# Splitting the weights of the mLSTM stage: seven subtractions moved from GpSimd to VectorE, and the modulation steps placed anew

## The reference

```
def mlstm_mixer(h, w_in, conv_w, b_if, hnorm_g, w_out):
    proj = einsum('bsd,de->bse', h, w_in)               # 1024 qk, 1024 v, 1024 o, 16 gate columns
    qk = silu(causal_conv(qk, conv_w))                  # four taps
    q, k = split(qk, 2)
    i_pre, f_pre = split(gates + b_if, 2)
    log_f = log_sigmoid(f_pre)                          # running sums and maxima give the decay
    ...
    hh = num / max(abs(den), exp(-m_t))                 # per head, from q, k, v and the decay
    hh = rmsnorm(hh, hnorm_g) * sigmoid(o)
    return einsum('bse,ed->bsd', hh, w_out)
```

## Time and profile before

| | us |
|---|---|
| median of 3 runs | 2704.84 (2700.52 to 2705.44) |
| the profiled execution, its time | 2700.52 |
| its span | 2698.4 |
| PE busy | 2605.1 |
| DVE busy | 2003.0 |
| ACT busy | 1506.9 |
| POOL busy | 346.0 |

### The profile page before, as it was taken

One profiled execution on the slowest core, in us unless ns is written; L12 is line 12 of the kernel. 1 busy time (PEld: TensorE's weight loads), 2 busy tenths in 40 slices (PEclk: granted clock), 3 DMA queues, 4 the chain that ended last, 5 costly groups with the idle time before them and its releaser, 6 DMA issues.

```text
span 2698.4 us, 48877 instructions
## 1 busy us (share of the span) xinstructions
PE 2605.1 (97%) x17298; PEld 2380.5 (88%) x17298; DVE 2003.0 (74%) x3797; ACT 1506.9 (56%) x2604; POOL 346.0 (13%) x190
## 2 busy tenths in 40 slices
PE   5999999999999999899999999999999999999998
PEld 4779999999888888789999999888888889888897
DVE  6768957888888876568857888666666776677766
ACT  3455557766565656455557766665664544463443
POOL 3107600000000002607600000000000111002000
PEclk9999999999999999999999999999999999999999
DMA  6844574444788874424574444555555345542553
GB/s 223 292 144 164 195 230 147 141 147 148 267 277 278 280 257 142 143 70 165 195 231 141 146 144 149 187 195 193 191 193 190 105 166 194 180 156 96 194 187 132
DMA packets 134718, 490.78 MB, mean 182 GB/s; under 512 B 15521, under 2 KB 15609, under 8 KB 134273
## 3 DMA queue, kind: packets, MB, share of 16 engines
q1 hardware_dynamic: 131904, 480.31, 52.5%
q0 software_dynamic: 2624, 7.92, 0.9%
HBM read 487.12 MB, written 1.06 MB: 181 GB/s over the span
## 4 chain that ended last, share of the span: by engine, by line
PE 86%; DVE 7%; ACT 3%; DMA 2%; issue 2%; POOL 0%; SPq 0%; DVEq 0%; ACTq 0%; POOLq 0%
PE ps L221 77%; PE ps L1295 4%; DMA weight_ring<-in_stream 2%; ACT weight_split L236 1%; DVE weight_split L245 1%; PE ps L640 1%; DVE arena L1821 1%; DVE arena L632 1%; ACT arena L395 1%; PE ps L2402 1%; PE ps L1267 1%; DVE arena L1817 1%; POOL weight_split L245 0%; PE ps L1708 0%; PE ps L388 0%
## 5 line engine op out<-in xcount | busy, mean ns | idle before, releaser
L221 PE MATMUL ps<-hT_split,weight_split 128*128 128x256 f32 x9984 | 1260.1, 285 | 15.9 <-DVE hT_split L1831 4.7
L221 PEld LDWEIGHTS ps<-hT_split,weight_split 128*128 128x128 f32 x9984 | 1220.0, 192 | 27.5 <-issue 18.3
L245 DVE TENSOR_TENSOR weight_split<-weight_ring,weight_split 128x1024 fp32r<-128x1024 f32 x674 | 823.6, 1223 | 399.3 <-ACT weight_split L236 396.6
L236 ACT ACTIVATE weight_split<-weight_ring 128x1024 fp32r<-128x1024 f32 x800 | 848.0, 1061 | 230.5 <-PE ps L221 160.2
L221 PE MATMUL ps<-weight_split,hidden_split 128*128 128x512 f32 x3948 | 913.1, 390 | 7.3 <-DVE hidden_split L1561 3.6
L221 PEld LDWEIGHTS ps<-weight_split,hidden_split 128*128 128x128 f32 x3948 | 735.4, 188 | 160.0 <-issue 8.1
L245 POOL TENSOR_TENSOR weight_split<-weight_ring,weight_split 128x1024 fp32r<-128x1024 f32 x126 | 306.2, 2436 | 413.9 <-ACT weight_split L236 413.6
L1391 ACT ACTIVATE hidden_split<-arena 128x256 fp32r<-128x256 f32 (+1 forms) x256 | 176.3, 689 | 252.3 <-PE ps L221 252.3
L1383 ACT ACTIVATE arena<-ps 128x256 f32<-128x256 f32 (+18 forms) x248 | 126.9, 512 | 133.8 <-PE ps L221 133.8
L221 PE MATMUL ps<-weight_split,hT_split 128*128 128x512 f32 x660 | 159.9, 398 | 10.6 <-POOL weight_split L245 5.6
L1561 DVE TENSOR_TENSOR hidden_split<-arena,hidden_split 128x256 fp32r<-128x256 f32 x256 | 161.3, 631 | 0.0
(11 more groups left out here) (351 smaller groups left out, 1716.3 us busy)
## 6 DMA issues: line engine op xcount, KB each, us to landing
weight_ring<-in_stream SPq DMA_DIRECT2D x912, 512.0 KB, 3.3
x<-in_x SPq DMA_DIRECT2D x1, 1024.0 KB, 4.9
arena<-mlstm_m_rows POOLq DMA_DIRECT2D x1, 1024.0 KB, 6.4
arena<-in_ln_mix_g POOLq DMA_DIRECT2D x2, 512.0 KB, 4.9
arena<-in_ln_mix_b POOLq DMA_DIRECT2D x2, 512.0 KB, 6.1
arena<-in_ln_ffn_g POOLq DMA_DIRECT2D x2, 512.0 KB, 4.8
arena<-in_ln_ffn_b POOLq DMA_DIRECT2D x2, 512.0 KB, 6.4
out<-x SPq DMA_DIRECT2D x2, 512.0 KB, 2.6
```

What stands on the lines that cost most here:

```text
L221: mm = pe.matmul(out_, stationary(s_part), moving(m_part), start=start and n == 0, stop=stop and n == 2, skip_group_check=True)
L236: act.activation(wsplit[:, n % SPLITS, HIGH, :], ring[:, slot(POS[n]), :], ACT.Copy).then_inc(high_ready, 1)
L245: eng.tensor_tensor(w[:, REST, :], ring[:, slot(POS[n]), :], w[:, HIGH, :].bitcast(fp32), ALU.subtract).then_inc(split_ready, 1)
```

## The change

Three things are edited. POOL does the rests of s0 to s2 alone and then only issues the two DMAs of M. DVE does the rest of s3 inside the gate chain, before it waits for the logarithm, and in the convolution loop the rest of s(c+4) behind convolution c, with a16 and a17 behind the rests of s9 and s10. After the loop DVE does the rest of s12, a18, the decay argument, then rest of s13, a19, rest of s14, a20, rest of s15, a21, and a22 and a23 in a row.

```
-            rests_pool(ML_T, 4)
+            rests_pool(ML_T, 3)
 
             pool.wait_ge(ml_M_r, 1)
             pool.dma_start(ml_rows..., ml_M).then_inc(ml_M_out, 16)
-            for n in range(ML_T + 4, ML_T + 6):
-                rest(pool, n)
             pool.wait_ge(ml_M_out, 16)
             pool.dma_start(ml_Mb..., ml_rows.partition_broadcast(128)).then_inc(ml_M_in, 16)
-            for n in range(ML_T + 6, ML_T + 10):
-                rest(pool, n)
...
             after_dve(dve.tensor_scalar(ml_hnorm, ml_hnorm, 0.5, None, ALU.mult))
+            splits_until(dve, ML_T + 3)
+            rest(dve, ML_T + 3)
             dve.wait_ge(ml_ln, 1)
...
                 last.then_inc(ml_conv, 1)
-            ada_dve(16, ml_acc[:, 0])
-            dve.wait_ge(ml_M_in, 16)
-            dve.tensor_tensor(ml_arg, ml_Mb, ml_mask..., ALU.add).then_inc(ml_arg_r, 1)
+                rest(dve, ML_T + c + 4)
+                if c in (5, 6):
+                    ada_dve(11 + c, ml_acc[:, 0])
...
-            ada_dve(17, ml_acc[:, 0])
-            splits_until(dve, ML_T + 10)
-            for c in range(2, 8):
+            for c in range(4, 8):
                 rest(dve, ML_T + 8 + c)
-                ada_dve(16 + c, ml_acc[:, 0])
+                ada_dve(14 + c, ml_acc[:, 0])
+                if c == 4:
+                    dve.wait_ge(ml_M_in, 16)
+                    dve.tensor_tensor(ml_arg, ml_Mb, ml_mask..., ALU.add).then_inc(ml_arg_r, 1)
+            for a in (22, 23):
+                ada_dve(a, ml_acc[:, 0])
             weigh(0)
```

More of the change, by code:

```diff
@@ L1097, in mlstm_dve @@
                 last.then_inc(ml_conv, 1)
-            ada_dve(16, ml_acc[:, 0])
-            dve.wait_ge(ml_M_in, 16)
-            dve.tensor_tensor(ml_arg, ml_Mb, ml_mask.unsqueeze(1).broadcast_to([128, 8, T]), ALU.add).then_inc(ml_arg_r, 1)
+                rest(dve, ML_T + c + 4)
+                if c in (5, 6):
+                    ada_dve(11 + c, ml_acc[:, 0])
             def weigh(h):
@@ L1149, in two_out @@
                 out_rest(h + 1)
-            ada_dve(17, ml_acc[:, 0])
-            splits_until(dve, ML_T + 10)
-            for c in range(2, 8):
+            for c in range(4, 8):
                 rest(dve, ML_T + 8 + c)
-                ada_dve(16 + c, ml_acc[:, 0])
+                ada_dve(14 + c, ml_acc[:, 0])
+                if c == 4:
+                    dve.wait_ge(ml_M_in, 16)
+                    dve.tensor_tensor(ml_arg, ml_Mb, ml_mask.unsqueeze(1).broadcast_to([128, 8, T]), ALU.add).then_inc(ml_arg_r, 1)
+            for a in (22, 23):
+                ada_dve(a, ml_acc[:, 0])
             weigh(0)
```

## The result

| | before | after |
|---|---|---|
| median, us | 2705.14 (4 runs, 2700.52 to 2707.37) | 2731.96 (4 runs, 2729.67 to 2736.44) |
| profiled execution, time | 2700.52 | 2731.23 |
| its span | 2698.4 | 2729.0 |
| mean granted clock | 0.996 | 0.988 |

The ratio is 1.0106, with an interval of 1.0094 to 1.0118; it isn't the quotient of the two medians in the table, 1.0099, and the record lists 24 executions of the changed kernel in all, 2729.67 to 2738.98. The change costs 26.8 us between the medians and 30.6 us between the two profiled spans; the profiled execution of before lies 4.6 us under its median and that of after 0.7 us, which is the difference between the two figures.

A forecast was written before the change was run, and what follows sets the result against it. TensorE, busy 97% of the span, was taken as the bound, so s16's start sets the end. Late rest 32.1 plus clock 2.2 gave 34.3 us: 2734.8 from the profiled execution, 2739 from the median; forecast 2736, range 2720 to 2746.

The forecast's parts named there:

- the refill pair: v tiles: two refills issued in a row take 5.7 us until the second has landed, in each turn.
- the clock: PE's clock falls to 1.2 GHz after idle waits; hidden at the v tiles, on the path once at s16, +2.2 us.
- Rest of s3 and the gate chain: Before the loop: s3's rest on DVE starts at 54.0, the last scan falls to 0.68 us, first convolution at 57.8.
- The rule that the prediction took from the Trainium skill: Gate chain's scan: two-SBUF-input DVE instructions and SBUF-reading GpSimd instructions shut each other out; without it, sum 2.1 us higher.
- The convolution loop: Rests between convolutions on DVE come every 4.1, then 4.5 us; the rest of s11 is 8.4 us later.
- The ring: Loop: convolution, silu, high copy and rest wait on each other through DVE and ACT; period 4.1, then 4.5 us.
- The v tiles: s12 to s16: late modulation steps run the stream dry, 9.4 us a turn; s16's rest 32.1 us late.
- from s17 on the old order holds, at PE's pace: After s16: nothing later changes the delay, so s16's lateness reaches the kernel's end.
- The sum: Whole kernel: 32.1 us from s16's late rest plus 2.2 from the clock, 34.3 us on the profiled execution.
- The stream that catches up: Rival at the v tiles: refill pairs land nearly as fast as one, turns 7.0 us, 2723 to 2727; chance 0.15.
- a clock that stays low through the head stage: Rival: 1.2 GHz further into the heads, or a22 and a23 late too; +38 to +45, 2739 to 2750; chance 0.08.
- The faster case: Rival in the loop: ring doesn't bind, period under 2.93 us, PE's waits vanish, 2692 to 2697; chance 0.03.

The follow-up runs named there:

- The turned order on ACT: Changed kernel with ACT's high copy of tile c+4 put ahead of silu(c) in the convolution loop, modulation steps still late; 2723.27 us, ratio 1.0061.
- The experiment with the last wait filled: Changed kernel with 60 unread identity transposes behind tile s15 on PE, to keep PE busy until s16; 2733.24 us, ratio 1.0106.
- that kernel with the steps in place: Changed kernel with ACT's high copies ahead of silu and modulation steps at their old places relative to the split tiles; 2700.84 us, ratio 0.998.
- the late steps alone: Kernel before, rests of s0 to s9 still on POOL, with only the v tiles' modulation steps moved two tiles later; 2726.97 us, ratio 1.0072.

## Why the prediction was right

The forecast was 2736, the median is 2731.96, within the forecast's own range and on the predicted path. Two terms were too large, the refill pair by a little and the clock by most of its size. Step by step:

*Rest of s3 and the gate chain.* Right to half a microsecond: the rest starts at 54.48 (predicted 54.0), of which 0.38 is the stage's later start in this execution (its first high copy at 41.93 instead of 41.55); the scan takes 0.68 us as reckoned; the convolution starts at 58.28 (57.8). The rule that the prediction took from the Trainium skill, "SBUF — State Buffer", Who interferes with whom, agrees with the trace: 2.74 us beside POOL's subtraction and 0.68 without it.

*The convolution loop.* The ring was found and sized: 4.09 us a turn (4.1), then 4.65 (4.5), the rest of s11 at 93.93 (93.0). The 0.1 us a turn is from silu to high copy, 0.87 us with two silus where the prediction had 0.75. The turned order on ACT confirms the cause.

*The v tiles.* The mechanism was right, the turn a little too long: 8.69, 9.38, 8.53 and 9.56 us, in the mean 9.04, against 9.4. The refill pairs make it so. The issues are 0.6 us apart in one turn and 0.9 in another (100.0 and 100.6; 108.7 and 109.6), and the second tile is there 4.9 us (100.0 to 104.9) or 5.7 us (108.7 to 114.4) after the first issue. The prediction took the longer for all. (The page "DMA: Bandwidth & Descriptors" of the Trainium skill, Anatomy of one DMA, which is for DMAs issued from GpSimd, would give an estimated 4.4 us for such a pair; these refills, issued by SyncE, took 4.9 and 5.7.) Since s12 was 0.75 us later than reckoned, the two errors nearly cancel, which is luck: the rest of s16 is 31.4 us late (133.61 − 102.21), predicted 32.1.

*The clock.* This term was mis-sized. On s16 itself it was right, 5.25 us instead of 3.11. But the clock fell once more, at s18, which the sum doesn't have (4.62 us instead of 3.12), and neither delay lasts. PE's marks of the changed kernel, set against before:

| tile | before | after | later by |
|---|---|---|---|
| s16 | 103.58 | 134.99 | 31.41 |
| s17 | 108.70 | 142.25 | 33.55 |
| s18 | 117.13 | 149.89 | 32.76 |
| s19 | 122.96 | 157.22 | 34.26 |
| s22 | 140.52 | 174.77 | 34.25 |
| s23 | 148.69 | 180.74 | 32.05 |
| behind the heads | 155.18 | 187.23 | 32.05 |

Between s17 and s18, 0.8 us is made up: before, PE waited 0.54 us in that stretch for DVE's weighing of a head (L1107, up to 112.34), and in the changed kernel it doesn't. The rows at s23 show where the rest went: PE's timeline of before, and then of the changed kernel.

```profile
147.63 1.13 PE L921 MATMUL ps<-arena 8*128 8x256 f32 x4 [2.14 <-DVE arena L1132]
```

```profile
179.69 1.13 PE L917 MATMUL ps<-arena 8*128 8x256 f32 x4
180.74 3.14 PE L221 MATMUL ps<-hT_split,weight_split 128*128 128x256 f32 x24
...
187.23 5.74 PE L221 MATMUL ps<-weight_split,hidden_split 128*128 128x512 f32 x24
```

Before, PE waited 2.14 us here for DVE's reciprocal; slowed by the clock, it comes after DVE and waits no more. The prediction's step "from s17 on the old order holds, at PE's pace" failed here: it rested on a window that ends at 140.0, and the wait stands at 145.5 to 147.6. Of 3.6 us of clock (2.14 at s16 and 1.5 at s18), 0.64 is left (32.05 − 31.41), where the prediction has 2.2. The experiment with the last wait filled shows the same from the other side.

*The sum.* Predicted 34.3 on the profiled execution, measured 30.6 by span: 0.7 from the rest of s16, 1.6 from the clock, and 1.4 that is given back between 187 us and the end. The last is another clock. Before, it fell to 0.51 from 1143.5 to 1147.0. PE reaches the same work (the transposes at L1697, L1698 after the change) 32 us later, and there it is 1.00, from 1175.0 to 1178.5. The difference between the two timelines is 32.22 us at the head of that stretch (1143.04 and 1175.26) and 30.92 behind it (1148.06 and 1178.98). So 1.3 of the 1.4 us is a fall of the clock that before had and the changed kernel hasn't; why it hasn't is open, and nothing in the prediction stands for it. The remaining 3.8 us between span and medians comes from single executions lying apart: that of before was 4.6 us under its median. The forecast, set beside the first three executions' 2704.84, asks for 31.2 us where the medians give 26.8.

*The rivals.* The stream that catches up (turns of 7.0) didn't come; nor did a clock that stays low through the head stage, though it fell once more there, at s18. The faster case fell on the condition that the prediction named, a loop period of 4.1 instead of under 2.93; with the order on ACT turned the condition holds, and that kernel with the steps in place is in fact faster, by 0.2%.

## What to carry to other kernels

Before work is moved to another engine's queue, write down for each wait what stands ahead of the instruction that releases it: a copy behind a silu that waits for the very engine the copy is for costs a round trip a tile (4.1 instead of 2.6 us), and exchanging two lines in the other queue takes it away. In a stream with a fixed order, count the tiles between a slot's reader and the next tile that the others need: the slack is the ring's, and using it up costs the whole latency of a refill pair each turn, here 20 us for steps that had themselves plenty of idle time. A wait further down the chain absorbs a small delay, so follow the difference between the timelines beyond the first mark before counting it.

## What the runs showed of the hardware

The granted clock fell in places that the prediction hadn't named. In the loop it was 0.51 from 61.3 to 68.2, after a wait of 3.69 us before s4; this cost nothing, as the ring's period was longer than PE's work: PE waits again, 0.94 us, before s7 at 74.84. A wait doesn't tell by its length alone whether the clock falls: before s4 PE waited 3.21 us in the kernel before and in that with the late steps alone, and the 96 matmuls behind it took 11.74 us in one and 13.22 in the other. And it fell once with no wait at all in PE's row, from the window of the changed kernel at s18:

```profile
150.00:153.50 3.50, 3.50 (x19) 3.50 (x19) 2.86 (x4) 1.06 (x1) 0.00 (x0) 0.51 0.91 301
```

PE is busy 3.50 of 3.50 us at a clock of 0.51, and s18 takes 4.62 us. Ahead of it stand a tile, its head's products and 16 matmuls of one column (L640, 148.08 to 150.03), with no wait in between. With the last wait filled, the clock was 1.00 in this window. What made the difference is open.

A pair of 512 KB refills doesn't take twice the time of one. The page's 3.3 us is the median over all 912 refills, not a mean, and 3.3 to 3.7 us is what the first of the two pairs' tiles took. Both tiles were there after 4.9 or 5.7 us, the longer time where the second was issued 0.9 us behind the first instead of 0.6.
